# Two column sums moved from the closing group of a stage to the turn behind it, in a two-layer diffusion backbone

## The chip, the cores and the metric

The kernel runs on one core of a Trainium2 chip. The metric is the device time of one execution, in microseconds (us). A core has a matrix engine (TensorE, here PE), a vector engine (DVE), a scalar engine (ACT), GpSimd (POOL) and a sync engine (SP) that here issues all the large transfers. The engines run side by side and wait for each other through semaphores, counters that one instruction raises and another waits on. SBUF is the memory on the core; PSUM is the small memory into which PE writes, in 8 banks of 512 fp32 values per partition.

## The reference, cut to what matters

256 latent tokens of width 2048 go through two layers. Each layer has a mixer (the first Fourier and attention, the second a gated convolution) and an MLP. Each of these four sub-layers begins with a norm, modulated by six vectors that come from the conditioning vector `c`, and ends with a gated norm that is added to the stream:

```
sh_m, sc_m, gt_m, sh_f, sc_f, gt_f = split(silu(c) @ w_mod[l] + b_mod[l], 6)
ux = rmsnorm(x, g[0]) * (1 + sc_m) + sh_m
x  = x + gt_m * rmsnorm(mix(ux), g[1])
x  = x + gt_f * rmsnorm(relu(modulate(x, g[2], sh_f, sc_f) @ w1)**2 @ w2, g[3])
```

The weights are read once, 588 MB in all, of which `w_mod` is a third. `sh_f` (vector 3 of a layer, the shift of the MLP's norm) and `sc_f` (vector 4, its scale) are the ones that the change touches.

## The kernel before

**Large products.** A weight group is a strip of 2048 rows by 512 columns, cut into 8 slabs of 512 KB. For each slab SP starts the transfer into `raw` (4 slots), ACT rounds it into `whi` (L906), DVE forms the remainder `wlo` (L1272), and PE multiplies it with the high and low halves of the activations. So PE can begin a slab when its `lo_ready` count is there, and a slot is free again when PE has used it. An "MLP first" group gives transposed outputs (L520, L526). A "token group" (L595 to L597) gives token rows: per slab 6 products for token half a = 0 and 6 for a = 1.

**The closing group.** The last of the four groups of an output projection is called with `closing=True`. Its slabs 0 to 3 run as usual. Of slabs 4 to 7 it runs first all 24 products of half 0, then the 24 of half 1. While PE does half 1, ACT and DVE already take half 0 through the norm (`row_norm`).

**The turn.** Then the first group of the MLP begins with `turns`: PE transposes the scaled stream through the identity (L831, `turn_half`). Half 0 of the first two pairs goes first, then filler products into a bank that nobody reads (`keep_clock`, L824), then, once DVE has scaled half 1 (`first_scaled`), half 1, two more filler products, and the first slab. On the other side, `boundary` on DVE and ACT turns each pair of columns into scaled, shifted, split activations `u`: `shifted(b)` reads the transposed bank, multiplies by `der` and adds the shift in `vt`; `low(b)` (L1442) makes the low half, for which PE waits with its first slab.

**Conditioning vectors.** `w_mod` is read in units of half a vector (1024 columns, 16 slabs), in the order of `UNITS`. DVE adds each slab, times its value of silu(c), onto an accumulator `acc` (L1282, `unit_slab`; two accumulators, the unit's parity picks one). The sum over the 128 partitions is then made by POOL (L1919) for most units. For two units, 5 and 17 (`COLUMN_UNITS`), it is made by PE: `sum_columns` multiplies the 8 blocks of `acc` with a column of ones into bank 6 (L794), and `finish` on DVE adds the bias and writes `vt` (L1384). POOL then zeroes that accumulator (L1912). Unit 5 is the second half of layer 0's vector 3, and its slabs come in beside groups 0 to 2 of the attention output projection (`PG_WO`); unit 17 is the same for the convolution output projection (`PG_CO`). `mod_ready` counts finished units, in their order.

The three numbers `MOD_NEEDED` say how many units `boundary` waits for before it forms `der`. The order of everything is the order of the code on each engine.

The lines of the profile that the prediction speaks of are: L794 column sums, L824 filler, L831 transposes, L595 to L597 token products, L520 and L526 first-type products, L906 `whi`, L1272 `wlo`, L1282 unit slab, L1384 `finish` of a column unit, L1435 `shifted`, L1670 `x_piece`, L1699 scaling of the stream, L1442 `low`.

Of the kernel before, what the change touches and what calls it, by code (L numbers as in the profile page):

```python
# [37 lines left out]
PG_MLP = (9, 57)  # L38
# [4 lines left out]
def slab_of(pg):  # L43
# [3 lines left out]

UNITS = [(0, 4, 0), (0, 4, 1), (0, 3, 0), (0, 2, 0), (0, 2, 1), (0, 3, 1), (0, 5, 0),
         (1, 0, 0), (1, 0, 1), (1, 1, 0), (1, 1, 1), (1, 2, 0), (0, 5, 1), (1, 2, 1),
         (1, 3, 0), (1, 3, 1), (1, 4, 0), (1, 4, 1), (1, 5, 0), (1, 5, 1)]  # L50
MIX_UNITS = (2, 3)
LATE_UNIT, LATE_SLOTS = 4, 3
ACT_PAIRS = (1, 3, 5)
# [54 lines left out]
def backbone_program(nc, x_in, c_in, ctx_in, c_ctx, w_mod, b_mod, gains, att_w_in, sink, att_w_out,  # L108
                     conv_w_in, conv_w, conv_w_out, mlp_w1, mlp_w2, tables, out):
    with ExitStack() as ctx:  # L110
# [355 lines left out]
        def _(pe):  # L466
# [322 lines left out]
            def sum_columns(un):  # L789

                pe.wait_ge(m_used, first_slab(un) + UNIT)
                pe.wait_ge(mod_ready, un)
                for c in range(KC // 2):
                    last = pe.matmul(ps[:, 6, 2 * c:2 * c + 2], acc[:, un % 2, c * P:(c + 1) * P], ones[:, 0:2],  # L794
                                     start=True, stop=True)
                last.then_inc(columns_done, 1)
# [17 lines left out]
            for i in range(4):  # L814
                if i >= 2:
                    pe.wait_ge(sum_done, sums_before(PG_WO + i - 1))
                token_group(PG_WO + i, (PG_WO + i) % 2, u,
                            (out_waits, None, None, lambda s: sum_columns(U_WO) if s == 4 else None)[i], closing=(i == 3),
                            order=OUT_ORDER, src2=h)

            def keep_clock(bank, n):

                for _ in range(n):
                    pe.matmul(ps[:, bank, :], ident, tab[:, 0:512], start=True, stop=True)  # L824

            def turns(j, slot):

                def turn_half(b, a):
                    for c in range(2):
                        k = 2 * b + c  # L830
                        last = pe.transpose(ps[:, turn_bank(slot, b), c * T + a * P:c * T + (a + 1) * P],  # L831
                                            yt[:, a, k * P:(k + 1) * P], ident)
                    if a:
                        last.then_inc(u_t, 1)

                def turn(b):
                    if b % 2 == 0:
                        pe.wait_ge(x_scaled, 6 * j + b)
                    if b in (5, 7):
                        pe.wait_ge(act_shifted, 3 * j + (b - 3) // 2)  # L840
                    elif b >= 4:
                        pe.wait_ge(u_shifted, shifts_through(j, b - 4))
                    turn_half(b, 0)
                    turn_half(b, 1)

                def ahead(s):
                    if s == 0:
                        pe.wait_ge(first_scaled, 3 * j + 1)
                        turn_half(0, 0)
                        turn_half(1, 0)  # L850
                        keep_clock(4 * (1 - slot) + 3, 4)
                        for b in range(2):
                            pe.wait_ge(first_scaled, 3 * j + 2 + b)
                            turn_half(b, 1)
                        keep_clock(4 * (1 - slot) + 3, 2)
                    elif s == 1:
                        turn(2)
                        turn(3)
                    elif s < SL - 2:
                        turn(s + 2)  # L860
                return ahead
# [26 lines left out]
            for i in range(4):  # L888
                pe.wait_ge(sum_done, sums_before(PG_CO + i - 1))

                def slab_waits(s):
                    pe.wait_ge(conv_ready, s + 1)
                    if i == 3 and s == 4:
                        sum_columns(U_CO)
                token_group(PG_CO + i, (PG_CO + i) % 2, h, slab_waits, closing=(i == 3))
            mlp_groups(1)

# [2 lines left out]
        def _(act):  # L900
# [258 lines left out]
            def boundary(j, w0, shift):  # L1159


                slot = (w0 // SL + 1) % 2

                def shifted(b):
                    act.wait_ge(u_t, 8 * j + b + 1)
                    if b >= 2:
                        act.wait_ge(u_ready, 8 * (j + 1) + b - 1)
                    for c in range(2):
                        k = 2 * b + c
                        last = act.activation(mt[b % 2][:, c, :], two_tiles(turn_bank(slot, b))[:, c, :], ACT.Identity,  # L1170
                                              scale=der[:, k:k + 1], bias=vt[:, shift + k:shift + k + 1])
                    last.then_inc(act_shifted, 1)

                def high(b):
                    if b in ACT_PAIRS:
                        act.wait_ge(act_shifted, 3 * j + (b + 1) // 2)
                    else:
                        act.wait_ge(u_shifted, shifts_through(j, b))
                    act.activation(u[:, 2 * b:2 * b + 2, 0:T], mt[b % 2], ACT.Copy).then_inc(u_hi, 1)

                def scale_x(g):
                    for a in range(2):
                        cols = slice(g * GW, (g + 1) * GW)
                        act.wait_ge(rstd_ready, 4 + 4 * j + 2 * a)
                        act.wait_ge(x_step, 8 * j + 2 * g + a + 1)
                        act.activation(yt[:, a, cols], x[:, a, cols], ACT.Copy, scale=r_x[:, a:a + 1]
                                       ).then_inc(x_scaled, 1)

                act.wait_ge(gs_ready, j + 1)
                for b in (0, 2, 4):  # L1190
                    high(b)
                    shifted(b + 1)
                    if b:
                        hi(w0 + b + 2, (b + 2) % SLOTS)
                    high(b + 1)
                    if b == 0:
                        scale_x(1)
                        hi(w0 + 2, 2)
                    hi(w0 + b + 3, (b + 3) % SLOTS)
                    if b < 4:  # L1200
                        scale_x(b // 2 + 2)
                high(6)
                high(7)
# [64 lines left out]
        def _(dve):  # L1268
# [435 lines left out]

            def out_units(un):
                return lambda i: stage_units(un, 4, i, un % 2, True)
            last_stage(0, PG_WO, out_units(U_WO), slab_of(PG_MLP[0]), False, ((3,), (4,), (), (5,)))

            def boundary(j, scale, gain, shift, w0):

                dve.wait_ge(mod_ready, MOD_NEEDED[j])
                dve.scalar_tensor_tensor(out=der[:, :], in0=vt[:, scale:scale + KC], scalar=1.0,
                                         in1=gT[:, gain:gain + KC], op0=ALU.add, op1=ALU.mult).then_inc(gs_ready, 1)
                dve.wait_ge(gs_ready, j + 1)
                gs, sh = der[:, :].unsqueeze(2), vt[:, shift:shift + KC].unsqueeze(2)
                slot = (w0 // SL + 1) % 2
                n0 = 8 * (j + 1)

                def shifted(b):
                    dve.wait_ge(u_t, 8 * j + b + 1)  # L1720
                    if b >= 2:
                        dve.wait_ge(u_ready, n0 + b - 1)
                    shift_pair(n0 + b, gs, sh, mt[b % 2], two_tiles(turn_bank(slot, b)))

                def low(b):
                    if b in ACT_PAIRS:
                        dve.wait_ge(act_shifted, 3 * j + (b + 1) // 2)
                    else:
                        dve.wait_ge(u_shifted, shifts_through(j, b))
                    pair_low(n0 + b, mt[b % 2])  # L1730
                for b in range(0, PAIRS, 2):
                    shifted(b)
                    if b == 0:
                        x_piece(j, 1, 0)
                    low(b)
                    if b == 0:
                        x_piece(j, 1, 1)
                    else:
                        lo(w0 + b, b % SLOTS)
                    if b == 6:  # L1740
                        shifted(7)
                    low(b + 1)
                    lo(w0 + b + 1, (b + 1) % SLOTS)
                    if b < 4:
                        for a in range(2):
                            x_piece(j, b // 2 + 2, a)
# [142 lines left out]
            for t in range(4):  # L1889
                for j in range(3):  # L1890
# [5 lines left out]
                         (None, convolve(t), low_v(t))[j])  # L1896
                    if (3 * t + j) % 4 == 1:
                        finish(un - 1)
            last_stage(2, PG_CO, out_units(U_CO), slab_of(PG_MLP[1]), False, ((), (16,), (), (17,)))
            boundary(2, L1 + 4 * KC, G1 + 2 * KC, L1 + 3 * KC, slab_of(PG_MLP[1]))  # L1900
            mlp(1, U_MLP1, 0)

# [44 lines left out]

MOD_NEEDED = (6, 11, 18)  # L1950


def shape_tables():
# [47 lines left out]
```

## Time and profile before

| what | value |
|---|---|
| time, median of 3 runs | 2278.65 us (2277.66 to 2279.47) |
| the profiled execution's own time | 2279.34 us |
| its span (first to last instruction) | 2277.6 us |
| PE busy | 2210.6 us, 97% of the span |
| DVE busy | 1653.5 us, 73% |
| ACT busy | 1019.0 us, 45% |
| POOL busy | 99.5 us, 4% |
| transfers, mean | 260 GB/s |
| mean granted clock of PE | 0.987 |

The span plus what lies around it (1.74 us here) is the time. A matmul's end is modelled, and successive ones overlap, so the distance between two starts says more than one duration. In a timeline row stand the start, the length (of a row "xN", of all N together), engine, line, what is written and read, and in brackets how long the engine sat idle before and for whom. The granted clock is 1.00 at 2.4 GHz and 0.50 at 1.2 GHz.

### The profile page before, as it was taken

How to read it: one execution, taken by the hardware profiler on the slowest of the kernel's cores; microseconds unless marked ns; L12 is line 12 of the kernel's file. 1: busy time of each engine (PE TensorE's matmuls, PEld its weight loads, DVE VectorE, ACT ScalarE, POOL GpSimd, SP SyncE). 2: the span in 40 equal slices, each digit the busy share in tenths (PEclk: the TensorE clock that was granted, in tenths of full speed). 3: DMA queues.
4: the chain of work that ended last, by engine and by line, in shares of the span. 5: the costliest groups of instructions: out<-in, count | busy, mean ns of one | idle time of the engine just before them, and what ended most of it. 6: DMA issues, size and time to landing. Idle time of an engine off the chain costs nothing.

```text
span 2277.6 us, 30993 instructions
## 1 busy us (share of the span) xinstructions
PE 2210.6 (97%) x11363; PEld 1813.2 (80%) x11363; DVE 1653.5 (73%) x1784; ACT 1019.0 (45%) x1269; POOL 99.5 (4%) x32
## 2 busy tenths in 40 slices
PE   7899999999999999999989999999999999999998
PEld 3478568788888888888868888877888888888887
DVE  0266758788788888888989889987887654655565
ACT  3163544554344345344454444455444443443443
POOL 0000000001010110110101101100011000000000
PEclk8899999999999999999999999999999999999999
DMA  9966978588888878889867898895887666666764
GB/s 374 354 221 231 371 266 301 204 276 279 300 277 294 291 263 295 292 275 317 297 202 274 273 305 279 274 315 164 299 282 254 203 194 189 187 196 193 207 193 149
DMA packets 253896, 592.63 MB, mean 260 GB/s; under 512 B 18082, under 2 KB 18610, under 8 KB 253234
## 3 DMA queue, kind: packets, MB, share of 16 engines
q1 hardware_dynamic: 253746, 590.63, 77.0%
q8 instruction: 95, 1.56, 0.3%
q14 instruction: 55, 0.45, 0.1%
HBM read 588.46 MB, written 2.10 MB: 259 GB/s over the span
## 4 chain that ended last, share of the span: by engine, by line
PE 84%; DVE 6%; DMA 4%; ACT 3%; issue 3%; SPq 0%; DVEq 0%; ACTq 0%
PE ps L520 29%; PE ps L526 14%; PE ps L595 11%; PE ps L596 11%; PE ps L597 11%; DMA early<-in_w_mod_dram 2%; DVE wlo L1272 2%; PE ps L559 2%; ACT whi L906 1%; DMA mraw<-in_w_mod_dram 1%; DVE acc L1282 1%; PE ps L481 1%; DMA raw<-in_mlp_w_dram 1%; DVE fq L1435 0%; PE ps L687 0%
## 5 line engine op out<-in xcount | busy, mean ns | idle before, releaser
L1272 DVE TENSOR_TENSOR wlo<-raw,whi 128x1024 fp32r<-128x1024 f32 x712 | 903.9, 1274 | 422.6 <-ACT whi L906 421.6
L906 ACT ACTIVATE whi<-raw 128x1024 fp32r<-128x1024 f32 x712 | 750.8, 1058 | 938.6 <-PE ps L597 382.4
L520 PE MATMUL ps<-u,whi 128*128 128x512 f32 x2944 | 930.2, 397 | 13.7 <-DVE wlo L1272 9.8
L526 PEld LDWEIGHTS ps<-u,wlo 128*128 128x128 f32 x2944 | 554.5, 188 | 131.3
L526 PE MATMUL ps<-u,wlo 128*128 128x256 f32 x2944 | 579.7, 278 | 0.0
L595 PE MATMUL ps<-whi,h 128*128 128x512 f32 x1216 | 475.4, 391 | 3.9 <-DVE wlo L1272 3.9
L596 PE MATMUL ps<-wlo,h 128*128 128x512 f32 x1216 | 474.1, 390 | 0.0
L597 PE MATMUL ps<-whi,h 128*128 128x512 f32 x1216 | 474.1, 390 | 0.0
L520 PEld LDWEIGHTS ps<-u,whi 128*128 128x128 f32 x2944 | 449.9, 189 | 24.3 <-issue 13.1
L1282 DVE SCALAR_TENSOR_TENSOR acc<-mraw,cs,acc 128x1024 f32<-128x1024 f32 x240 | 306.9, 1279 | 4.4 <-DMA mraw<-in_w_mod_dram 4.2
L595 PEld LDWEIGHTS ps<-whi,h 128*128 128x128 f32 x1216 | 228.9, 188 | 52.9 <-DVE wlo L1272 5.7
L597 PEld LDWEIGHTS ps<-whi,h 128*128 128x128 f32 x1216 | 228.8, 188 | 48.0
L596 PEld LDWEIGHTS ps<-wlo,h 128*128 128x128 f32 x1216 | 228.9, 188 | 47.2 <-issue 0.2
L1919 POOL PARTITION_ALL_REDUCE red<-acc x13 | 85.0, 6537 | 1170.0 <-DVE acc L1282 496.2
L1004 ACT ACTIVATE tmp<-ps 128x512 f32<-128x512 f32 x92 | 53.7, 595 | 34.3 <-PE ps L526 34.3
L559 PE MATMUL ps<-early,junk 128*32 128x512 f32 x192 | 43.3, 707 | 16.2 <-DMA early<-in_w_mod_dram 16.2
L1212 ACT ACTIVATE h<-fq 128x512 fp32r<-128x512 f32 x64 | 39.6, 634 | 32.2 <-DVE fq L1763 32.2
L1756 DVE TENSOR_TENSOR fq<-ps,tmp 128x512 f32<-128x512 f32 x64 | 43.0, 685 | 9.5 <-ACT tmp L1004 9.4
L1295 DVE SCALAR_TENSOR_TENSOR acc<-mraw,cs,acc 128x1024 f32<-128x1024 f32 x30 | 38.5, 1283 | 12.1 <-DMA mraw<-in_w_mod_dram 12.0
L1774 DVE TENSOR_TENSOR h<-fq,h 128x512 fp32r<-128x512 f32 x64 | 41.2, 684 | 0.0
L1763 DVE SCALAR_TENSOR_TENSOR fq<-fq 128x512 f32<-128x512 f32 x64 | 41.1, 683 | 0.0
L559 PEld LDWEIGHTS ps<-early,junk 128*32 128x32 f32 x192 | 6.7, 118 | 36.3 <-DMA early<-in_w_mod_dram 22.6
(195 smaller groups left out, 1268.0 us busy)
## 6 DMA issues: line engine op xcount, KB each, us to landing
raw<-in_mlp_w_dram SPq DMA_DIRECT2D x512, 512.0 KB, 4.7
mraw<-in_w_mod_dram SPq DMA_DIRECT2D x272, 512.0 KB, 5.5
early<-in_w_mod_dram SPq DMA_DIRECT2D x96, 512.0 KB, 7.0
raw<-in_conv_w_in_dram SPq DMA_DIRECT2D x96, 512.0 KB, 5.4
raw<-in_att_w_in_dram SPq DMA_DIRECT2D x40, 512.0 KB, 4.6
raw<-in_att_w_out_dram SPq DMA_DIRECT2D x32, 512.0 KB, 6.3
raw<-in_conv_w_out_dram SPq DMA_DIRECT2D x32, 512.0 KB, 6.0
raw<-in_w_mod_dram SPq DMA_DIRECT2D x16, 512.0 KB, 7.1
```

Source lines behind the costliest of these rows:

```text
L520: return pe.matmul(ps[:, 4 * slot + m, :], whi[:, s % SLOTS, cols], src[:, k, :], start=(k == 0), stop=False)
L526: return pe.matmul(ps[:, 4 * slot + m, 0:T], wlo[:, s % SLOTS, cols], src[:, k, 0:T], start=False, stop=(k == KC - 1))
L559: last = pe.matmul(ps[tile:tile + 32, (0, 2, 0, 6)[hv] + n, :], crs[:, k, :], start_slab(w)[:, n * 512:(n + 1) * 512], start=(k < 4), stop ...
L595: pe.matmul(o, high, whi[:, s % SLOTS, cols], start=first, stop=False)
L596: pe.matmul(o, high, wlo[:, s % SLOTS, cols], start=False, stop=False)
L597: last = pe.matmul(o, low, whi[:, s % SLOTS, cols], start=False, stop=final)
L906: act.activation(whi[:, s, :], raw[:, s, :], ACT.Copy).then_inc(hi_ready, 1)
L1004: act.activation(tmp[half][:, :, :], right(slot, half), ACT.Copy).then_inc(b_copied, 1)
L1272: dve.tensor_tensor(wlo[:, s, :], raw[:, s, :], whi[:, s, :], ALU.subtract).then_inc(lo_ready, 1)
L1282: dve.scalar_tensor_tensor(out=a, in0=src, scalar=cs[:, bass.ds(k, 1)], in1=a, op0=ALU.mult, op1=ALU.add).then_inc(m_used, 1)
L1756: dve.tensor_tensor(tsum[half], left((pg0 + i) % 2, half), tmp[half][:, :, :], ALU.add).then_inc(sum_done, 1)
L1919: pool.partition_all_reduce(red[:, :], acc[:, un % 2, :], P, RADD).then_inc(unit_summed, 1)
```

## The change

The column sums of units 5 and 17 leave slab 4 of the closing group. They go into the turn, behind the transposes of half 0, and two of the four filler products there go. DVE's `finish` for these units moves from before the closing group's row work to behind `shifted(0)` in `boundary`. Since `der` is formed before that, the scale (vector 4) must be complete: in layer 0 its units come first already; in layer 1, units 14 to 17 are swapped so that the scale's two halves are 14 and 15 and the shift's are 16 and 17. PE waits for the finished unit before the first slab (bank 6 belongs to that group), ACT before the first pair that uses the second half of the shift.

```diff
-         (1, 3, 0), (1, 3, 1), (1, 4, 0), (1, 4, 1), (1, 5, 0), (1, 5, 1)]
+         (1, 4, 0), (1, 4, 1), (1, 3, 0), (1, 3, 1), (1, 5, 0), (1, 5, 1)]
...
                 token_group(PG_WO + i, (PG_WO + i) % 2, u,
-                            (out_waits, None, None, lambda s: sum_columns(U_WO) if s == 4 else None)[i], closing=(i == 3),
+                            (out_waits, None, None, None)[i], closing=(i == 3),
                             order=OUT_ORDER, src2=h)
...
                         turn_half(0, 0)
                         turn_half(1, 0)
-                        keep_clock(4 * (1 - slot) + 3, 4)
+                        if j in LATE_COLUMNS:
+                            sum_columns(LATE_COLUMNS[j])
+                        keep_clock(4 * (1 - slot) + 3, 2 if j in LATE_COLUMNS else 4)
                         for b in range(2):
                             pe.wait_ge(first_scaled, 3 * j + 2 + b)
                             turn_half(b, 1)
                         keep_clock(4 * (1 - slot) + 3, 2)
+                        if j in LATE_COLUMNS:
+                            pe.wait_ge(mod_ready, LATE_COLUMNS[j] + 1)
...
                 def slab_waits(s):
                     pe.wait_ge(conv_ready, s + 1)
-                    if i == 3 and s == 4:
-                        sum_columns(U_CO)
...
                 def shifted(b):
+                    if b == PAIRS // 2 + 1 and j in LATE_COLUMNS:
+                        act.wait_ge(mod_ready, LATE_COLUMNS[j] + 1)
                     act.wait_ge(u_t, 8 * j + b + 1)
...
-            last_stage(0, PG_WO, out_units(U_WO), slab_of(PG_MLP[0]), False, ((3,), (4,), (), (5,)))
+            last_stage(0, PG_WO, out_units(U_WO), slab_of(PG_MLP[0]), False, ((3,), (4,), ()))
...
                     shifted(b)
                     if b == 0:
+                        if j in LATE_COLUMNS:
+                            finish(LATE_COLUMNS[j])
                         x_piece(j, 1, 0)
...
-            last_stage(2, PG_CO, out_units(U_CO), slab_of(PG_MLP[1]), False, ((), (16,), (), (17,)))
+            last_stage(2, PG_CO, out_units(U_CO), slab_of(PG_MLP[1]), False, ((), (16,), ()))
...
-MOD_NEEDED = (6, 11, 18)
+MOD_NEEDED = (5, 11, 17)
+LATE_COLUMNS = {0: U_WO, 2: U_CO}
```

On PE, in the closing group of the attention output projection, this is what stands where slab 3 ends and slab 4 begins (`acc` is the unit's accumulator, `tab` holds the ones and the identity):

```order
@@ -1163,5 +1163,4 @@
 L596 MATMUL ps<-wlo,h 128x512
 L597 MATMUL ps<-whi,h 128x512
-L794 MATMUL ps<-tab,acc 128x2 x8
 L595 MATMUL ps<-whi,u 128x512
 L596 MATMUL ps<-wlo,u 128x512
```

The eight column products are gone there, and slab 4 follows slab 3 directly.

On PE, at the turn that follows (`y` is the scaled stream; the rows with `tab` alone are filler):

```order
@@ -1213,5 +1212,6 @@
 L597 MATMUL ps<-whi,u 128x512
 L831 MATMUL ps<-tab,y 128x128 x4
-L824 MATMUL ps<-tab 128x512 x4
+L794 MATMUL ps<-tab,acc 128x2 x8
+L824 MATMUL ps<-tab 128x512 x2
 L831 MATMUL ps<-tab,y 128x128 x4
 L824 MATMUL ps<-tab 128x512 x2
```

The eight column products stand behind the first four transposes, and two filler products follow them instead of four. The convolution output projection changes in the same way.

## Rows read from the trace of the kernel before

**Rows 1.** Timeline of PE, closing group of the attention output projection, and turn.

```profile
426.38 0.39 PE L597 MATMUL ps<-whi,h 128*128 128x512 f32 x1
428.82 2.30 PE L794 MATMUL ps<-tab,acc 128*128 128x2 f32 x16 [2.06 <-issue]
430.99 0.77 PE L595 MATMUL ps<-whi,u 128*128 128x512 f32 x1
...
437.08 0.40 PE L597 MATMUL ps<-whi,u 128*128 128x512 f32 x1
...
444.80 0.60 PE L831 MATMUL ps<-tab,y 128*128 128x128 f32 x4
445.23 3.60 PE L824 MATMUL ps<-tab 128*128 128x512 f32 x8
449.71 0.70 PE L831 MATMUL ps<-tab,y 128*128 128x128 f32 x4 [0.88 <-DVE y L1699]
```

**Rows 2.** Timeline of DVE, the same closing group.

```profile
426.31 1.22 DVE L1272 TENSOR_TENSOR wlo<-raw,whi 128x1024 fp32r<-128x1024 f32 x1
427.44 1.28 DVE L1282 SCALAR_TENSOR_TENSOR acc<-mraw,cs,acc 128x1024 f32<-128x1024 f32 x1
...
430.12 1.23 DVE L1272 TENSOR_TENSOR wlo<-raw,whi 128x1024 fp32r<-128x1024 f32 x1
```

**Rows 3.** Timeline of ACT, the same closing group.

```profile
429.03 1.06 ACT L906 ACTIVATE whi<-raw 128x1024 fp32r<-128x1024 f32 x1 [3.82 <-DMA raw<-in_att_w_out_dram]
...
432.35 0.19 ACT L1127 ACTIVATION_READ_ACCUMULATOR fq<-y 128x1 f32 x1
```

**Rows 4.** Timeline of PE, closing group of the convolution output projection, and turn.

```profile
1529.95 0.39 PE L597 MATMUL ps<-whi,h 128*128 128x512 f32 x1
...
1534.01 3.54 PE L794 MATMUL ps<-tab,acc 128*128 128x2 f32 x16 [3.67 <-DVE acc L1282]
...
1551.00 0.60 PE L831 MATMUL ps<-tab,y 128*128 128x128 f32 x4
```

**Rows 5.** Timeline of DVE, that closing group.

```profile
1531.34 1.22 DVE L1272 TENSOR_TENSOR wlo<-raw,whi 128x1024 fp32r<-128x1024 f32 x1
...
1535.01 1.22 DVE L1272 TENSOR_TENSOR wlo<-raw,whi 128x1024 fp32r<-128x1024 f32 x1
```

**Rows 6.** Timeline of PE, closing group of layer 0's MLP, and turn.

```profile
1158.20 0.50 PE L595 MATMUL ps<-whi,h 128*128 128x512 f32 x1 [1.85 <-DVE wlo L1272]
...
1161.87 0.50 PE L595 MATMUL ps<-whi,h 128*128 128x512 f32 x1 [2.02 <-DVE wlo L1272]
...
1168.81 0.60 PE L831 MATMUL ps<-tab,y 128*128 128x128 f32 x4
```

**Rows 7.** Stretches: length, busy per engine, then clock, DMA share, GB/s.

```profile
430.00:431.00 1.00, 1.00 (x8) 1.00 (x7) 0.94 (x3) 1.00 (x4) 0.00 (x0) 0.60 1.00 367
1160.00:1162.00 2.00, 0.13 (x1) 0.13 (x2) 1.82 (x3) 2.00 (x8) 0.00 (x0) 1.00 0.84 294
1532.00:1533.00 1.00, 0.00 (x0) 0.00 (x0) 1.00 (x2) 0.00 (x0) 0.00 (x0) 0.85 0.85 266
```

**Rows 8.** Timeline of PE, column sums of units 0 to 2 (L755).

```profile
345.10 1.84 PE L755 MATMUL ps<-tab,red 128*128 128x2 f32 x16
346.80 0.48 PE L595 MATMUL ps<-whi,h 128*128 128x512 f32 x1
```

**Rows 9.** Timelines of DVE and ACT at the first turn.

```profile
451.17 0.74 DVE L1670 SCALAR_TENSOR_TENSOR x<-y,st,x 128x512 f32<-128x512 f32 x1
452.08 0.69 DVE L1442 TENSOR_TENSOR u<-fq,u 128x512 fp32r<-128x512 f32 x1 [0.17 <-ACT u L1179]
...
451.35 0.63 ACT L1179 ACTIVATE u<-fq 128x512 fp32r<-128x512 f32 x1 [2.49 <-DVE fq L1435]
```

**Rows 10.** Timeline of POOL and DVE: a memset of an accumulator beside a remainder.

```profile
1098.87 0.95 POOL L1922 MEMSET acc<- 128x1024 f32 x1
...
1099.43 1.21 DVE L1272 TENSOR_TENSOR wlo<-raw,whi 128x1024 fp32r<-128x1024 f32 x1
```

## The prediction

> **What bounds the kernel now.** I read the busy shares first: PE is busy for 2210.6 of 2277.6 us, so what lengthens PE's own stream, or leaves it empty, is time. Then I read PE's timeline around the moved instructions (L794), and beside it DVE's and ACT's, to see what each wait on PE ends on and what would be late next.
>
> In the closing group of the attention output projection, PE finishes slab 3 with the product that starts at 426.38, then stands idle until 428.82, then spends 2.17 us on the column sums, and goes on with slab 4 at 430.99 [rows 1]. The idle time is marked "issue", but DVE's row ends it: the last unit slab runs from 427.44 to 428.72 [rows 2], and the sums need it. Slab 4 itself needs nothing of this. In the convolution output projection the same place costs more: idle from 1530.2 to 1534.01, then 3.4 us of sums at the low clock [rows 4].
>
> There is a third cost. In the first of the two places the granted clock falls during the idle time and the sums (0.60 between 430 and 431) [rows 7]. The 14 products from 430.99 to 437.08 take 6.09 us; the 34 from there to 444.80 take 7.72 us, 0.227 each [rows 1]. At that pace the 14 would take 3.18 us, so the fall costs 2.9 us. In the second place the clock falls before the sums even begin, between 1532 and 1533 (0.85) [rows 7].
>
> **Part 1: the sums leave the closing group.** Without them PE runs slabs 4, 5 and 6 straight behind slab 3: 18 products of 0.227 us are 4.09 us. In the attention projection that is 426.61 + 4.09 = 430.70. Slab 7 is late next: its remainder ends at 430.12 + 1.23 = 431.35 [rows 2]. It cannot come earlier, since its rounding on ACT waited 3.82 us for its transfer [rows 3], and that transfer was released by DVE's progress on slab 4, not by PE. So a wait of 0.7 us takes the place of the old one, and slab 7's six products for half 0 and the 24 for half 1 follow.
>
> What these 30 products take after such a wait is seen in the closing group of layer 0's MLP, which has no column sums: there PE waits 1.85 and 2.02 us for two remainders, and from the product at 1161.87 to the first transposes at 1168.81 pass 6.94 us, at full clock [rows 6, 7]. From the end of a remainder to PE's start I allow 0.05 us. So the turn begins at 431.35 + 0.05 + 6.94 = 438.34 instead of 444.80: **6.46 us earlier**.
>
> In the convolution projection: 1530.18 + 4.09 = 1534.27. The remainder of slab 6 is there at 1531.34 + 1.22 = 1532.56, before PE wants it at 1532.9; that of slab 7 ends at 1536.23 [rows 5]. So PE waits 2.0 us, and the turn begins at 1536.23 + 0.05 + 6.94 = 1543.22 instead of 1551.00: **7.78 us earlier**. I take the clock as staying up across this wait, since two waits of 1.85 and 2.02 us with only six products between them did not lower it (1.00 between 1160 and 1162) [rows 6, 7].
>
> The norm of half 0 has to keep up. It runs beside the 24 products of half 1 both before and after; it begins when half 0 ends and the distance to PE's next need stays the same, 24 products. ACT's squares of the group before end at 432.54 [rows 3], and half 0 would end at about 431.40 + 6 x 0.227 + 0.2 = 432.96, so they are just not in the way (before, the room was 7 us).
>
> **Part 2: the sums in the turn.** There PE has spare time: after the transposes of half 0 it fills 3.60 us with eight filler records and then is still idle for 0.88 us, until DVE has scaled half 1 [rows 1]. New there are 16 records of sums; four filler records go. At full clock the sums of another unit took 346.80 - 345.10 = 1.70 us to the next product [rows 8]. Four filler records are half of 3.60, less the overlap at the end: 1.71 us. So the filling is as long as before (3.41 us), and the 0.88 us stay. At the low-clock price of 3.4 us [rows 4] the filling would be 1.7 us longer and overrun the room by 0.8 us. I take 0, since all of the first turn runs at full clock, and keep 0.8 us per turn as the upper end.
>
> DVE's `finish` (0.16 us long) now stands between `shifted(0)` and the first `x_piece`. The next step, `low(0)`, is the one that PE's first slab waits for. It already waits 0.17 us behind `x_piece` for ACT's rounding (451.35 to 451.98) [rows 9]. So the added 0.18 us fits that gap almost exactly; I take 0.05 us per turn, at most 0.2. PE's new wait, ACT's new wait and the swap of units cost nothing: PE's first slab waits for `low(0)` anyway, which DVE runs after `finish`; ACT's wait is for its fifth pair, microseconds later; each swapped unit loads as many bytes in the same places, and the scale is complete a group earlier than it was. SP waits for finished units only behind slab 7 of the MLP's first group, long after `finish`.
>
> POOL's memset of the accumulator moves too, from the closing group, where DVE was idle, to the turn, where DVE's short norm steps are on the path. A memset of this size beside a remainder left the latter at 1.21 us, its usual length [rows 10]; by that it costs 0. If it blocked DVE for its whole 0.95 us, that would be 0.95 us per turn, 1.9 in all; I keep that as an end only. The Trainium skill (SBUF — State Buffer, "Who interferes with whom") says that a DVE instruction with two SBUF inputs is not disturbed by a GpSimd instruction that only writes, but that one in a two-port mode, which `tensor_scalar` can enter, blocks and is blocked. The row shows the first half of this; by the second half, DVE's small `tensor_scalar` steps could wait for the memset, and the sum would be up to 1.9 us less; no row shows such a pair.
>
> The accumulator is needed again only by the unit after next, some 60 us later, so the later zeroing delays no one.
>
> **The sum.** 6.46 + 7.78 - 2 x 0.05 = 14.1 us. Against the profiled execution's own 2279.34 us that is 2265.2; that execution lay 0.69 us over the median, so 2264.5 us. Everything behind each turn should only move, since transfers resume with the progress of DVE in the turn.
>
> **Rivals.**
>
> *The clock falls at a new place.* For it: before, the low clock came after 2.4 us of idleness in the convolution projection, and a new wait there is 2.0 us; in the turn, sums that keep PE thinly loaded follow transposes. Against: the MLP's closing group [rows 6, 7]. Price: 2.9 us for a fall in that closing group; in the turn two filler products at half clock, 1.7 us late, less the 0.88 of room, and two more behind the second transposes, 1.7 late again, less what PE waits there for `low(0)` (until 452.77, from 449.71 + 0.54 + 1.71 = 451.96, 0.8 us) [rows 1, 9]: about 1.8 us per turn. One fall in the closing group gives 2267.4; with both turns too, 2271.0. The Trainium skill (TensorE: Matmul & The Clock Gate, "Part 4: PE-mode transpose") says that transposes don't count as busy for the clock, which speaks against the new turn, in which sums stand directly behind them. The traced turns, with transposes between fillers, stay at full clock; should the rule tip the new one, the sum would be the 1.8 us per turn less that the rows give.
>
> *The next wait is longer than I read.* Slab 7's remainder, or the norm of half 0 behind ACT's squares, comes later than in the trace of before, because everything now hangs on it. For it: both have little room left (0.7 us, 0.4 us). Against: neither depends on PE. Price if each is 2 us late: 2264.5 + 4 = 2268.5.
>
> *The other side: the low clock holds on past the turn.* The sums and two fewer fillers let the clock fall in each turn, and the MLP's first group, where PE stops again and again for DVE, doesn't bring it back. Each microsecond of product work at half clock then costs one. It decides once more than 14.1 / 2 = 7 us are lost per boundary; were the whole group of eight slabs at half clock (8 products of 512 and 8 of 256 columns per slab; from 0.227 us for 512 columns I estimate 2.7 us a slab, 22 us in all), it would lose 20 each: 2264.5 + 40 = 2304. Against: the one fall before was over at 437.08, 6 us after products resumed.
>
> *The wait does not go.* If PE waited for the unit's last slab at slab 4 for another reason, only the order would have changed, and the time would be about 2278.7.
>
> **How the numbers follow.** Forecast 0.72; clock falls at one or more new places 0.15; next wait longer 0.08; other side 0.03; wait does not go 0.02. The forecast's own range is 2262.5 to 2266.5 (the ends above are costs of 0.8, 0.2 and 0.95 per turn; below, a PE that resumes up to 1 us sooner in each place). With the first two rivals up to 2270 less than 2 in 10 is left out: 2262 to 2270. About 0.2% is what a measurement of this kernel can tell from no change, 4.6 us; so faster than 2274.1 is 0.95, the same 0.02, slower 0.03.
>
> **What would show it.** In the profile after: slab 4 of both closing groups starts 0.23 us behind slab 3; PE waits there once, 0.7 and 2.0 us, for L1272; the clock is 1.00 throughout; the turn starts about 6.5 us earlier in the first place and 14.2 us earlier in the second; the sums last 1.8 us there and the wait for half 1 is still 0.9 us. Wrong would be: a clock under 1.00 at either place, sums of over 2.3 us in the turn, or a first slab that starts later behind the turn's start than 8.1 us (444.80 to about 452.9 before, from the end of `low(0)` [rows 9]).

## The result

The changed kernel takes 2267.46 us (median of 5 runs, 2265.29 to 2269.61), the kernel before 2278.29 us in the same comparison (5 runs, 2277.66 to 2279.47): a ratio of 0.9950 with a 95% interval from 0.9940 to 0.9961. By the ratio 11.4 us are saved (8.9 to 13.7), by the difference of the medians 10.8, against a forecast of 14.1, which lies outside that interval. The time lies 3.0 us over the predicted 2264.5, inside the stated range from 2262 to 2270 but outside the forecast's own, narrower one (2262.5 to 2266.5).

Two later comparisons of the same kernel, with more runs of the kernel before, gave 0.9945 (0.9932 to 0.9958) and 0.9939 (0.9925 to 0.9953): 12.5 and 13.9 us (by the medians 12.9 and 12.1). In them the kernel before ran from 2275.0 to 2282.8 us. The first three runs shown made it look steadier than it is.

The profiled execution took 2269.61 us (span 2267.8), the slowest of the five.

**The first place.** PE's timeline in the closing group of the attention output projection, and at the turn, which answers to [rows 1] (start, length, engine, line, written and read, idle time before):

```profile
432.56 0.50 PE L595 MATMUL ps<-whi,u 128*128 128x512 f32 x1 [0.74 <-DVE wlo L1276]
...
439.54 0.60 PE L831 MATMUL ps<-tab,y 128*128 128x128 f32 x4
439.97 1.84 PE L794 MATMUL ps<-tab,acc 128*128 128x2 f32 x16
441.68 1.96 PE L824 MATMUL ps<-tab 128*128 128x512 f32 x4
444.43 0.70 PE L831 MATMUL ps<-tab,y 128*128 128x128 f32 x4 [0.79 <-DVE y L1703]
444.96 1.88 PE L824 MATMUL ps<-tab 128*128 128x512 f32 x4
447.63 0.70 PE L520 MATMUL ps<-u,whi 128*128 128x512 f32 x2 [0.79 <-DVE u L1446]
```

The old wait, the sums and the slow products are gone. One wait of 0.74 us for slab 7's remainder is left, and from 432.56 to the turn at 439.54 pass 6.98 us. In the turn the sums and two filler products take 3.67 us from the start of the first to the end of the last (the four filler products of before: 3.60), and PE still waits 0.79 us for half 1. The first slab follows 8.09 us behind the turn's start; before it was 8.12.

DVE there, which answers to [rows 2] and [rows 9] (same columns):

```profile
431.28 1.22 DVE L1276 TENSOR_TENSOR wlo<-raw,whi 128x1024 fp32r<-128x1024 f32 x1
...
442.47 0.16 DVE L1414 RECIPROCAL st<-st 128x1 f32<-128x1 f32 x1 [0.23 <-ACT st L939]
442.67 0.27 DVE L1696 TENSOR_SCALAR st<-st 128x1 f32<-128x1 f32 x1
...
445.89 0.15 DVE L1388 TENSOR_TENSOR vt<-ps,small 128x8 f32<-128x8 f32 x1
445.96 0.74 DVE L1674 SCALAR_TENSOR_TENSOR x<-y,st,x 128x512 f32<-128x512 f32 x1
446.79 0.69 DVE L1446 TENSOR_TENSOR u<-fq,u 128x512 fp32r<-128x512 f32 x1
```

and POOL's memset, which answers to [rows 10]:

```profile
441.88 0.95 POOL L1918 MEMSET acc<- 128x1024 f32 x1 [92.10 <-PE ps L794]
```

The moved `finish` (L1388) delays the next instruction by 0.07 us only, and `low(0)` (L1446), for which PE waits, begins 7.25 us behind the turn's start; before it was 7.28 [rows 9]. The memset, from 441.88 to 442.83, covers DVE's reciprocal at 442.47 and the first 0.16 us of the scalar step at 442.67; they last 0.16 and 0.27 us, as they do in the turn of before, where no memset runs.

**The second place.** PE in the closing group of the convolution output projection, which answers to [rows 4]:

```profile
1530.98 0.50 PE L595 MATMUL ps<-whi,h 128*128 128x512 f32 x1 [0.61 <-DVE wlo L1276]
...
1534.65 0.50 PE L595 MATMUL ps<-whi,h 128*128 128x512 f32 x1 [2.01 <-DVE wlo L1276]
...
1541.59 0.60 PE L831 MATMUL ps<-tab,y 128*128 128x128 f32 x4
```

PE waits 0.61 us for slab 6 as well, which I had not foreseen (I had it ready 0.3 us before PE), and 2.01 us for slab 7. The first wait costs nothing here, since the second one follows it. The turn comes 6.94 us after that.

**Where the missing gain went in this execution.** PE in the closing group of layer 0's MLP, which the change doesn't touch, and which answers to [rows 6]:

```profile
1154.26 0.50 PE L595 MATMUL ps<-whi,h 128*128 128x512 f32 x1 [2.00 <-DVE wlo L1276]
1154.59 0.55 PE L596 MATMUL ps<-wlo,h 128*128 128x512 f32 x1
1154.94 0.63 PE L597 MATMUL ps<-whi,h 128*128 128x512 f32 x1
...
1157.93 0.80 PE L595 MATMUL ps<-whi,h 128*128 128x512 f32 x1 [1.08 <-DVE wlo L1276]
...
1166.53 0.60 PE L831 MATMUL ps<-tab,y 128*128 128x128 f32 x4
```

and the stretches there (length, busy time per engine, granted clock, DMA share, GB/s):

```profile
1152.00:1154.00 2.00, 0.26 (x2) 0.00 (x0) 1.97 (x4) 0.00 (x0) 0.00 (x0) 1.00 0.97 317
1154.00:1156.00 2.00, 1.74 (x5) 1.42 (x6) 2.00 (x3) 1.30 (x2) 0.00 (x0) 0.67 1.03 390
1156.00:1158.00 2.00, 0.92 (x3) 0.20 (x2) 1.84 (x3) 2.00 (x7) 0.00 (x0) 0.50 0.86 304
```

The clock has fallen behind the 2.00 us wait, and the last 30 products take 8.60 us instead of 6.94: 1.7 us. Between the first turn and the second 3.0 us are lost in all. The other 1.3 us are a late last remainder: it ended 3.95 us earlier than in the profile of before (1157.87 against 1161.82), while the first turn was 5.26 us earlier. The start of the kernel had also lost 0.9 us, before anything that the change touches: the first column sums of units 0 to 2 began at 335.55, in the profile of before at 334.62. Behind the third turn nothing more is lost: from there to the end pass 726.2 us, before 726.6.

### The profile page after: what moved, and what is told of

It is laid out like the page before. It is cut to its first block, busy times and chain, and to the rows that moved or that the text cites. A ratio compares the mean times of both kernels' runs of the same rounds, so it can differ in the third digit from the quotient of the medians.

```text
span 2267.8 us, 30977 instructions
## 1 busy us (share of the span) xinstructions
PE 2205.1 (97%) x11355; PEld 1808.2 (80%) x11355; DVE 1652.5 (73%) x1784; ACT 1018.3 (45%) x1269; POOL 99.4 (4%) x32
## 4 chain that ended last, share of the span: by engine, by line
PE 84%; DVE 6%; DMA 4%; ACT 3%; issue 2%; SPq 1%; DVEq 0%; ACTq 0%
PE ps L520 29%; PE ps L526 14%; PE ps L595 11%; PE ps L596 11%; PE ps L597 11%; DVE wlo L1276 2%; PE ps L559 2%; DMA early<-in_w_mod_dram 2%; DMA mraw<-in_w_mod_dram 1%; ACT whi L908 1%; DVE acc L1286 1%; DMA raw<-in_mlp_w_dram 1%; PE ps L481 1%; DVE x L1674 1%; PE ps L687 0%
## 5 line engine op out<-in xcount | busy, mean ns | idle before, releaser
L1299 DVE SCALAR_TENSOR_TENSOR acc<-mraw,cs,acc 128x1024 f32<-128x1024 f32 x30 | 38.5, 1282 | 12.1 <-DMA mraw<-in_w_mod_dram 12.1
```

## The experiments

Each number below is a median; ratios are to the kernel before on the same chip, with 95% intervals. The interval of each is about 0.13% on either side (3 us), so the profiles carry most of the weight. One quantity is read from all: the time from the end of the last remainder of a closing group (DVE) to the first transposes of the turn (PE). It leaves out what happened earlier in the execution.

| kernel | attention out | layer 0 MLP | convolution out | time |
|---|---|---|---|---|
| before | 13.45 | 6.99 | 14.77 | 2278.65 |
| before again | 12.01 | 7.01 | 13.77 | 2279.7 |
| changed | 7.04 | 8.66 | 7.00 | 2267.46 |
| changed again | 7.00 | 7.00 | 8.62 | 2266.51 |
| changed, third | 7.02 | 8.78 | 8.64 | 2267.38 |
| filler in waits | 7.00 | 7.00 | 7.23 | 2264.37 |
| filler in waits again | 7.00 | 7.02 | 7.73 | 2266.92 |
| one block summed | 6.99 | 6.98 | 7.02 | 2267.85 |
| sums at slab 7 | 7.48 | 6.98 | 6.99 | 2266.63 |
| first place only | 6.98 | 6.99 | 14.52 | 2274.15 |
| second place only | 13.55 | 8.84 | 7.00 | 2270.89 |
| full filler | 6.99 | 8.62 | 7.00 | 2269.19 |

The three columns in the middle are us in one profiled execution. Where the sums stand at slab 4, PE has hardly begun slab 4, or not yet, when that remainder ends; the distance there holds nearly all 48 products of slabs 4 to 7, some of them slow, and not 30.

**The changed kernel again** (no edit).

> The changed kernel once more, for a second profile. Theory A: the changed places gain 14 us as forecast, and about 3 us of it were lost in the profiled execution in the closing group of layer 0's MLP, which the change doesn't touch (weight slabs 1.3 us later, and a low clock that cost 1.7 us); that loss comes and goes. Then the two changed places again begin their turn 7.0 us after the last remainder, and the time lies between 2264 (no low clock) and 2269 (low clock). Theory B: the loss belongs to the change (the shifted phase brings it each time): the low clock is there again, and the time is 2267 to 2269.

Measured: 2266.51 us (2265.48 to 2267.65), ratio 0.9945 (0.9932 to 0.9958). The low clock was not in the MLP's closing group this time, but in the convolution's (PE's timeline and the stretches):

```profile
1530.99 0.50 PE L595 MATMUL ps<-whi,h 128*128 128x512 f32 x1 [2.02 <-DVE wlo L1276]
1531.33 0.39 PE L596 MATMUL ps<-wlo,h 128*128 128x512 f32 x1
1531.56 0.40 PE L597 MATMUL ps<-whi,h 128*128 128x512 f32 x1
1531.80 0.58 PE L595 MATMUL ps<-whi,h 128*128 128x512 f32 x1
1532.18 0.63 PE L596 MATMUL ps<-wlo,h 128*128 128x512 f32 x1
```

```profile
1530.00:1531.00 1.00, 0.01 (x1) 0.01 (x1) 0.94 (x1) 1.00 (x5) 0.00 (x0) 1.00 0.94 361
1531.00:1532.00 1.00, 1.00 (x4) 0.87 (x5) 0.00 (x0) 0.99 (x4) 0.00 (x0) 0.92 0.56 217
1532.00:1533.00 1.00, 1.00 (x3) 0.75 (x3) 0.00 (x0) 0.00 (x0) 0.00 (x0) 0.50 0.74 121
```

PE had waited 0.87 and 2.02 us with six products between, and the clock fell 0.8 us after work had resumed (0.92 in the stretch from 1531: it was low for the last 0.16 us of it). So the loss moves from place to place; theory B's fixed loss in the MLP is refuted by the 7.00. The median lies in theory A's range and 0.5 us below theory B's.

**Filler in the waits of the closing groups.**

```diff
                     for s in range(SL - SLOTS, SL):
+                        keep_clock(7, (fill or {}).get(s, 0))
                         slab_waits_all(s)
                         last = products(s, 0)
...
+                                    fill={6: 2, 7: 2} if l == 0 else None)
...
-                token_group(PG_CO + i, (PG_CO + i) % 2, h, slab_waits, closing=(i == 3))
+                token_group(PG_CO + i, (PG_CO + i) % 2, h, slab_waits, closing=(i == 3), fill={7: 2})
```

> The changed kernel with two filler products (0.86 us each) ahead of the waits for slabs 6 and 7 in the closing group of layer 0's MLP, and ahead of slab 7 in that of the convolution output projection. Theory A: the waits there are 2.0 us, so 1.7 us of filler fit in, the clock stays at 1.00 in every execution, and the time is 2264 to 2266 with less spread; 1.5 to 2 us under the changed kernel's median. Rival: the clock isn't what costs the time, and the filler is late where the wait is shorter (0.6 or 1.1 us): 0.5 to 1.5 us slower than the changed kernel.

Measured: 2264.37 us (2261.64 to 2267.70), ratio 0.9938 (0.9926 to 0.9950). The profile shows the filler in place and full clock in all three groups. In the MLP's group (PE; L600 is the product line here, L584 the filler):

```profile
1149.01 1.88 PE L584 MATMUL ps<-tab 128*128 128x512 f32 x4
1151.17 0.50 PE L600 MATMUL ps<-whi,h 128*128 128x512 f32 x1 [0.28 <-DVE wlo L1278]
...
1152.66 1.88 PE L584 MATMUL ps<-tab 128*128 128x512 f32 x4
1154.83 0.50 PE L600 MATMUL ps<-whi,h 128*128 128x512 f32 x1 [0.29 <-DVE wlo L1278]
```

The median is 2.1 us under the changed kernel's in the same comparison, but the intervals overlap, and the executions spread over 6.1 us against 2.2.

**One of eight blocks summed in the turn, four fillers kept.**

```diff
-                            sum_columns(LATE_COLUMNS[j])
-                        keep_clock(4 * (1 - slot) + 3, 2 if j in LATE_COLUMNS else 4)
+                            sum_columns(LATE_COLUMNS[j], 1)
+                        keep_clock(4 * (1 - slot) + 3, 4)
```

> The changed kernel with one of the eight blocks summed in each of the two turns (seven eighths of the shift's second half are left out) and the four filler products of before. It prices the sums in the turn. Forecast's step (they replace filler at equal length, 1.7 us, and cost nothing): the same time as the changed kernel within 0.5 us, first slab 8.1 us behind the turn's start. Rival (sums in the turn delay it): 1 to 3 us faster than the changed kernel.

Measured: 2267.85 us (2263.30 to 2270.13), ratio 0.9950 (0.9938 to 0.9963), no faster than the changed kernel. In the profile the first slab follows the turn's start by 8.12 and 8.11 us, in those of the changed kernel by 8.02 to 8.12, and in those of before by 8.12 and 8.13. So the sums cost nothing against filler of the same length. `finish` and the memset are in both versions; that they cost nothing either is read from the same distance in the kernel before.

**The kernel before with the sums ahead of slab 7.**

```diff
                     for s in range(SL - SLOTS, SL):
+                        if s == 7 and un is not None:
+                            sum_columns(un)
                         slab_waits_all(s)
                         last = products(s, 0)
```

Units, turn and `finish` are those of the kernel before; the calls at slab 4 are taken out.

> The kernel before, with one edit: the sums stand ahead of slab 7 of the closing groups instead of slab 4; turn and order of units as before. If the sums cost mainly by the wait for the last unit slab and by the clock, as I read, they now fall into PE's new wait for slab 7: 1.0 us late in the attention projection (1.7 us of sums against 0.7 us of wait), 0 to 0.3 in the convolution projection: 13 us under before, about 1 us over the changed kernel (2265.5 to 2268.5). The clock may fall after a wait filled with sums only; then 2.9 us more. Rival (the products themselves are the cost, wherever they stand in the group): 2271 to 2273.

Measured: 2266.63 us (2265.78 to 2267.52), ratio 0.9945 (0.9932 to 0.9958): the same ratio as the changed kernel's in this comparison, without its turn, and below the 2271 to 2273 of the rival. PE in both places:

```profile
432.39 0.39 PE L597 MATMUL ps<-whi,u 128*128 128x512 f32 x1
432.62 1.84 PE L796 MATMUL ps<-tab,acc 128*128 128x2 f32 x16
434.32 0.49 PE L595 MATMUL ps<-whi,u 128*128 128x512 f32 x1
```

```profile
1529.88 1.84 PE L796 MATMUL ps<-tab,acc 128*128 128x2 f32 x16
1532.02 0.50 PE L595 MATMUL ps<-whi,h 128*128 128x512 f32 x1 [0.30 <-DVE wlo L1272]
```

Three slabs later the unit's accumulator is complete when PE comes to it (1.4 us before in the first place, 0.5 us in the second), the sums take 1.70 us at full clock, and most of it lies in PE's wait for slab 7: 0.5 us too long in the first place, 0.3 us too short in the second. At slab 4 the wait, the sums and the slow products together cost some 12 to 13 us in the two places; at slab 7 the same products cost 0.5 us. So the cost was the wait for the unit's last slab and the low clock that came with it, not the products or their being in the group.

**The kernel before again** (no edit).

> The kernel before once more, for a second profile to set beside the first. Both places should again show the wait, the sums and the low clock: turns 13.4 us and 17.3 us behind the start of the product after the sums or more exactly 444.8 and 1551 within 2 us. Theory A (the closing group of layer 0's MLP falls to the low clock by chance, change or no change): the stretch between first and second turn is 724 us without a fall and 726 to 727 with one, in this kernel too. Theory B (the change brings it): 724.0 again, as in the first profile.

Measured: 2279.7 us over 12 runs (2275.82 to 2285.09), ratio 0.9998 (0.9989 to 1.0007). The clause on the distance from the sums to the turn was put wrongly (12.4 and 13.5 us were measured from the product behind the sums); the turns came at 444.54 and 1549.29, as expected. In the first place (PE):

```profile
427.54 0.39 PE L597 MATMUL ps<-whi,h 128*128 128x512 f32 x1
430.16 2.09 PE L794 MATMUL ps<-tab,acc 128*128 128x2 f32 x16 [2.23 <-issue]
432.11 0.77 PE L595 MATMUL ps<-whi,u 128*128 128x512 f32 x1
```

and in the MLP's closing group (stretches):

```profile
1157.00:1159.00 2.00, 0.16 (x1) 0.16 (x1) 2.00 (x4) 0.00 (x0) 0.00 (x0) 0.95 0.97 331
1159.00:1161.00 2.00, 2.00 (x5) 1.61 (x6) 1.97 (x3) 1.89 (x4) 0.00 (x0) 0.50 1.06 390
```

and, in the second place, the sums again (they begin at 1533.30, behind an idle time of 3.88 us):

```profile
1532.00:1533.00 1.00, 0.00 (x0) 0.00 (x0) 1.00 (x2) 0.00 (x0) 0.00 (x0) 1.00 1.02 340
1534.00:1535.00 1.00, 1.00 (x8) 1.00 (x8) 1.00 (x3) 1.00 (x4) 0.00 (x0) 0.63 1.01 377
```

The low clock is in the MLP's closing group of the kernel before too. Here it lay ahead of slab 7, where PE would have waited anyway (that wait shrank to 0.74 us), so it cost nothing there (7.01). Between the first two turns pass 724.9 us, more than the 724.0 of theory B and less than the 726 to 727 of theory A with a fall. So the fall itself does not need the change. In the second place the clock was still full at the end of the idle time and fell 1.0 us into the sums, where in the first profile it had fallen 2.4 us into the idle time [rows 7].

**First place only**, and **second place only**. The first has `LATE_COLUMNS = {0: U_WO}` and for the convolution everything as before (units, sums at slab 4, `finish`); the second has `LATE_COLUMNS = {2: U_CO}` and the swap of units, and for the attention everything as before.

```diff
-LATE_COLUMNS = {0: U_WO, 2: U_CO}
+LATE_COLUMNS = {0: U_WO}
```

> Only the attention output projection's place is changed; the convolution's place and the order of units are as before. Forecast's step: 6.5 us under before (ratio 0.9972), first turn at 437 to 440, third turn still with the wait, the sums at the low clock and 14 slow products. Rival (the two places share one gain, given back by transfers in between): 3 to 4 us.

Measured: 2274.15 us (2271.73 to 2277.38), ratio 0.9978 (0.9966 to 0.9990), 5.0 us saved (2.3 to 7.7). First turn at 437.80, the second place as before:

```profile
1528.21 3.54 PE L794 MATMUL ps<-tab,acc 128*128 128x2 f32 x16 [4.31 <-DVE acc L1288]
1531.62 0.77 PE L595 MATMUL ps<-whi,h 128*128 128x512 f32 x1
```

> Only the convolution output projection's place is changed, with the swap of units 14 to 17. Forecast's step: 7.8 us under before (ratio 0.9966); 6.1 if the clock falls in PE's new 2.0 us wait, as in the second profile of the changed kernel. Rival (gains given back): 4 us.

Measured: 2270.89 us (2269.60 to 2276.29), ratio 0.9963 (0.9950 to 0.9976), 8.4 us saved (5.5 to 11.4). Together 13.4 us, against 11.4 to 13.9 for both at once: within these intervals the two gains add up, and the rival of a gain given back between them (about 4 us for this one) lies below the interval. The rival figure for the first alone (3 to 4 us) is not excluded by its time; the table's 13.45, 12.01 and 13.55 against 7.0 exclude it in the profile. Note the 8.84 in the MLP: a low clock at the same place with the first place unchanged.

**Full filler beside the sums.**

```diff
-                        keep_clock(4 * (1 - slot) + 3, 2 if j in LATE_COLUMNS else 4)
+                        keep_clock(4 * (1 - slot) + 3, 4)
```

> The changed kernel with the four filler products of before kept beside the sums in both turns, 1.71 us more of PE work per turn. By the room that the profiles show (0.8 us of waiting for half 1, then 0.8 us for the low half of the first pair) each turn's second transposes come 0.9 us late and the first slab with them or a little less: 0.2 to 0.9 us per turn, so 0.3 to 1.8 us over the changed kernel. Rival (the turn has no real room, PE's own stream sets it): 1.7 us per turn, 3.4 us.

Measured: 2269.19 us (2264.72 to 2270.79), ratio 0.9946 (0.9933 to 0.9960). The turn (PE):

```profile
439.44 0.60 PE L831 MATMUL ps<-tab,y 128*128 128x128 f32 x4
439.87 1.84 PE L794 MATMUL ps<-tab,acc 128*128 128x2 f32 x16
441.58 3.68 PE L824 MATMUL ps<-tab 128*128 128x512 f32 x8
445.10 0.60 PE L831 MATMUL ps<-tab,y 128*128 128x128 f32 x4
445.53 1.88 PE L824 MATMUL ps<-tab 128*128 128x512 f32 x4
448.25 0.70 PE L520 MATMUL ps<-u,whi 128*128 128x512 f32 x2 [0.84 <-DVE u L1446]
```

The wait for half 1 is gone, and the first slab comes 8.81 us behind the turn instead of 8.09: 0.7 us per turn. The room of 0.8 us leaves 0.9 of the 1.7 us of added work, so this is within the 0.2 to 0.9 us expected, and the rival of 1.7 us per turn is excluded by the profile. By the profile, the change would cost 1.4 us more in its two turns without taking out two fillers; the times don't resolve this (ratio 0.9946, like the changed kernel's).

**The changed kernel a third time, and filler in the waits again**, side by side.

> The changed kernel a third time, beside the version with filler in the waits. Nine profiles so far say: from the end of the last remainder to the turn 6.9 to 7.0 us where the clock stays up and 8.5 to 8.6 where it has fallen, in each of the three closing groups by chance. Expected: again 7.0 or 8.6 in each, a time of 2265 to 2269, and 11 to 13 us under before.

Measured: 2267.38 us (2263.62 to 2268.34), ratio 0.9939 (0.9925 to 0.9953), 12.1 us under before by the medians and 13.9 by the ratio, so at the upper end of what I expected or above it. The clock fell in two of the three closing groups (8.78 and 8.64).

> The version with filler in the waits once more, in one call with the changed kernel. If the low clock in closing groups is what the changed kernel still loses now and then (1.6 us each), this one shows 7.0 us and full clock in all three closing groups again, and a median 1 to 2.5 us under the changed kernel's. Rival (its advantage in the first call was the scatter of executions): medians within 0.5 us.

Measured: 2266.92 us (2263.40 to 2267.50), ratio 0.9942 (0.9929 to 0.9956). The profile kept full clock in all three groups again, but the median is only 0.5 us below the changed kernel's, the end of the rival's range. In the convolution's group filler was late by 0.7 us (7.73), since there was less to wait for than in the profile from which it was sized. The clock stayed up in all four groups with filler in the two profiles. It also stayed up in 9 of 16 without, so four are few to show that filler is the reason. Whether it makes the kernel faster is not shown either; of the versions run, none is shown to beat the changed kernel.

## Why the prediction was right, and where it was off

**The wait, the sums and the slow products leave the closing group: right, and the size of the first place too.** I forecast 6.46 us. Read from remainder to turn, the first place took 13.45, 12.01 and 13.55 us in three profiles where it was unchanged, and 6.98 to 7.04 us in the eight profiles with the change there (sums at slab 7 aside). The mean gain is 6.0 us. The profile on which I argued had one of the two long ones; in the other profile of the kernel before the sums ran in 2.09 us instead of 2.30 and fewer products ran slow.

**The new wait for slab 7: right.** 0.7 and 2.0 us were forecast, 0.74 and 2.01 measured. The 6.94 us for 30 products was exact where the clock stayed up.

**The second place: over-sized.** "I take the clock as staying up across this wait." It stayed up in the first profile (7.00) and fell in the two others of the changed kernel (8.62, 8.64). This is the step of the sum that did not hold. I had rested it on one execution of the MLP's closing group, in which two such waits had left the clock alone [rows 6, 7]. The kernel before itself shows a fall there in its second profile. So that row was one draw and not a rule. The rival for it had a chance of 0.15 and a price of 2.9 us; the runs show a fall somewhere in all three profiles of the changed kernel, at 1.6 to 1.8 us. The base was off as well: 14.77 us in my profile, 13.77 and 14.52 in two others. With the means, 14.35 before and 8.09 in the three profiles of the changed kernel, the second place gains 6.3 us and not 7.8. Three more profiles have the same instructions in that group (one block summed, second place only, full filler), and in all three the clock stayed up (7.00 to 7.02). Over the six the mean is 7.55 and the gain 6.8, so it is the size of this loss that is uncertain, not that it occurs.

**The sum.** 6.0 + 6.3 = 12.3 us (12.8 with the six profiles), against 11.4, 12.5 and 13.9 measured in three comparisons. The forecast of 14.1 lies within the intervals of the last two, and 0.4 us outside that of the first. That the time fell into the stated range is in part luck: the room above 2266.5 was there for the two rivals. The measured 2267.46 all but equals the 2267.4 of the rival with one fall, but in its profile the fall was not in either of the two places for which the rival was priced. The forecast's own upper end was drawn too low by its own costs: 0.8, 0.2 and 0.95 us per turn, taken together, would give 2268.4, and 2266.5 holds only the last of them. Low clock in the MLP's closing group (1.7 us) is a third part, which I had not priced at all: "Everything behind each turn should only move" did not hold for that group. It cost time in two of three profiles of the changed kernel and in neither of the two of before, but it did so too with the first place unchanged; twelve profiles are too few to say whether the change makes it more frequent.

A fourth part may be a gain given back between the first turn and the MLP's last remainder. That stretch took 717.0 to 717.9 us in the three profiles with the first place unchanged and 717.6 to 718.4 in the eight with it changed, 0.6 us more in the mean. What causes this was not tried, and by so few profiles it is not settled.

**The turn: right.** The sums took 1.84 us, sums and fillers together 3.67 us against 3.60 before, and the wait for half 1 was 0.79 us (forecast 0.9). One block instead of eight changed nothing, and two more fillers cost 0.7 us. `finish` cost 0.07 us on DVE and nothing on PE. The clock was never below 1.00 in a turn of the changed kernel, so the risk that I gave the new turn by the Trainium skill (TensorE: Matmul & The Clock Gate, "Part 4: PE-mode transpose") did not show here.

**The memset beside DVE's steps: right at zero.** The wait of a `tensor_scalar` that I had feared by the Trainium skill (SBUF — State Buffer, "Who interferes with whom") did not show: the step beside the memset took 0.27 us, as without it. Whether a step of 128x1 enters a two-port mode at all, no run here shows.

**What I said would show it.** Of my signs of being wrong the first profile has none; the two later ones have one of them, a clock under 1.00 in the convolution's group. The turn did not come 14.2 us earlier in the second place, but 9.41 in the profiled execution. The first turn had lost 1.2 us (6.46 forecast, 5.26 found), 0.9 of it at the kernel's start; the stretch to the second turn lost 3.0 (1.7 to the clock, 1.3 to later slabs); the stretch from there to the third took 375.06 us instead of 382.19, 0.65 short of the forecast 7.78. What delays single slabs by a microsecond from run to run was not tried; the transfers were busy for 0.86 to 1.06 of the stretches shown up to the last waits of these groups.

One thing ahead of the prediction needs putting right: of a slab's buffers, PE frees those of `whi` and `wlo`. The slot in `raw`, into which the transfer goes, is free as soon as DVE has made the remainder, as the prediction has it.

## What to carry to other kernels

An instruction that waits for a slow producer should stand where its result is first needed, or inside another wait, not at the first place where it may stand: the same eight small products, with their wait and the slow products behind them, cost some 6 to 7 us each time at slab 4, and 0.5 us and nothing three slabs later. Price such a step with the wait, the instructions and the clock that comes after, and then look at what is late next. A profile is one draw: a stretch that kept the full clock across a wait of 2 us once can lose it in the next run, as the MLP's and the convolution's groups did here, so a forecast that rests on it needs a second profile or a wider price.

## What the runs showed of the hardware that was not expected

- Over the twelve profiles, 16 closing groups had no sums and no filler ahead of slabs 6 and 7, and a longest wait there of 1.5 to 2.2 us. In 9 of them the clock stayed at 1.00, in 7 it went to 0.50, with the same instructions in the group. A fall cost 1.6 to 1.8 us in the 30 products that follow, where it cost anything. In the attention projection's group, where the one wait was 0.5 to 1.1 us, it fell in none of the eight profiles with the first place changed.
- The distance from idleness to the fall differs from run to run. In the convolution's group of the kernel before the clock fell 2.4 us into an idle time of 3.7 us in one profile, and 1.0 us behind the end of an idle time of 3.9 us in the other. In the second profile of the changed kernel it fell 0.8 us after work had resumed.
- Eight products of 2 columns (16 records) took 1.84 us at full clock and 3.54 us at half: they scale with the clock although each streams only 2 columns. Each also loads a block of 128x128 as its weights; in the first turn the 16 loads took 1.87 us:

```profile
439.86 1.87 PEld L794 LDWEIGHTS ps<-tab,acc 128*128 128x128 f32 x16
```

- A memset on POOL of 0.95 us did not lengthen the small DVE steps beside it (0.16 and 0.27 us).
